# Softmax attention with unnormalised probabilities: the reciprocal row sums travel through DRAM and scale the output as it leaves PSUM

## The reference

```
def attend(qblk):                      # 8 heads, 1024 queries, 1024 keys
    s = jnp.einsum('bhqd,bhkd->bhqk', qblk, k_t).astype(jnp.float32) * scale
    p = jax.nn.softmax(s, axis=-1)
    return jnp.einsum('bhqk,bhkd->bhqd', p.astype(v_t.dtype), v_t)
...
o_b = o_b.transpose(1, 0, 3, 2, 4).reshape(B, S, MLA_HEADS * MLA_V)
```

## Time and profile before

| | before |
|---|---|
| median of 3 runs | 1935.23 us |
| lowest, highest | 1934.19, 1937.03 us |
| the profiled execution's own time | 1936.58 us |
| its span in the trace | 1934.7 us |
| PE busy | 1885.0 us (97%) |
| DVE busy | 1388.8 us (72%) |
| ACT busy | 1066.4 us (55%) |
| chain that ended last | PE 91%, DVE 5%, ACT 2% |

### The profile page before, as it was taken

How to read it: one execution, slowest core, us unless ns; L and a number is a source line. 1 busy time by engine, 2 the same in 40 slices (tenths; PEclk the granted TensorE clock), 3 DMA queues, 4 the chain that set the end, 5 groups by cost and what they waited for, 6 DMA issues and landing times.

```text
span 1934.7 us, 27125 instructions
## 1 busy us (share of the span) xinstructions
PE 1885.0 (97%) x9427; PEld 1598.3 (83%) x9427; DVE 1388.8 (72%) x1941; ACT 1066.4 (55%) x1768; POOL 135.8 (7%) x147
## 2 busy tenths in 40 slices
PE   8999999999999999999999999995999999999998
PEld 8988888888878888888888888884788888888886
DVE  4578777777855656556866348746799898998986
ACT  6576565655552434344534123324677777877775
POOL 1021111011000000000000000000000101001010
PEclk9999999999999999999999999997999999999999
DMA  6110000000321202021353553534999999999993
GB/s 209 44 43 7 23 18 23 23 18 26 121 66 33 64 25 66 22 77 65 120 176 131 178 192 109 175 142 181 359 400 400 391 401 393 396 400 390 399 391 77
DMA packets 147482, 327.58 MB, mean 169 GB/s; under 512 B 18080, under 2 KB 72736, under 8 KB 147232
## 3 DMA queue, kind: packets, MB, share of 16 engines
q1 hardware_dynamic: 141600, 309.59, 43.0%
q0 software_dynamic: 4752, 16.78, 3.4%
q10 hardware_dynamic: 1040, 0.00, 0.0%
HBM read 287.92 MB, written 38.40 MB: 169 GB/s over the span
## 4 chain that ended last, share of the span: by engine, by line
PE 91%; DVE 5%; ACT 2%; issue 1%; DMA 1%; POOL 1%; SPq 0%; DVEq 0%; ACTq 0%; POOLq 0%
PE ps L1108 24%; PE ps L1110 24%; PE ps L1109 24%; PE ps L1097 7%; PE ps L1195 3%; PE ps L1403 1%; PE ps L1234 1%; PE ps L1233 1%; PE ps L1415 1%; PE ps L1387 1%; PE ps L1413 1%; DVE affT L2571 1%; DMA xs<-in_x 1%; DVE top_v L2564 0%; DVE pT_lo L1719 0%
## 5 line engine op out<-in xcount | busy, mean ns | idle before, releaser
L1719 DVE TENSOR_TENSOR w_lo<-w_raw,w_hi 128x1024 fp32r<-128x1024 f32 x384 | 442.7, 1219 | 54.8 <-ACT w_hi L3173 54.6
L3173 ACT ACTIVATE w_hi<-w_raw 128x1024 fp32r<-128x1024 f32 x384 | 371.1, 1053 | 0.4 <-PE ps L1110 0.4
L1108 PE MATMUL ps<-w_hi,xeT_hi 128*128 128x512 f32 x512 | 201.2, 393 | 1.0 <-DVE w_lo L1719 0.9
L1110 PE MATMUL ps<-w_hi,xeT_lo 128*128 128x512 f32 x512 | 199.7, 390 | 0.0
L1109 PE MATMUL ps<-w_lo,xeT_hi 128*128 128x512 f32 x512 | 199.2, 389 | 0.0
L1719 DVE TENSOR_TENSOR d_lo<-d_raw,d_hi 128x1024 fp32r<-128x1024 f32 (+1 forms) x66 | 67.1, 1027 | 124.5 <-ACT d_hi L2814 119.9
L1108 PE MATMUL ps<-hT_parts,d_hi 128*128 128x512 f32 x368 | 145.3, 395 | 0.0
L1110 PE MATMUL ps<-hT_parts,d_lo 128*128 128x512 f32 x368 | 143.9, 391 | 0.0
L1109 PE MATMUL ps<-hT_parts,d_hi 128*128 128x512 f32 x368 | 143.8, 391 | 0.0
L1015 POOL TENSOR_TENSOR stat<-stat,minus_half 128x4 f32<-128x4 f32 (+3 forms) x56 | 54.3, 971 | 1176.5 <-DVE stat L1716 1176.4
L1954 DVE TENSOR_REDUCE row_max<-ps 128x1 f32<-128x1024 f32 x64 | 78.3, 1224 | 79.1 <-PE ps L1234 79.0
(11 more groups left out here) (451 smaller groups left out, 4363.3 us busy)
## 6 DMA issues: line engine op xcount, KB each, us to landing
w_raw<-in_w_gate_e SPq DMA_DIRECT2D x128, 512.0 KB, 7.4
w_raw<-in_w_up_e SPq DMA_DIRECT2D x128, 512.0 KB, 7.1
w_raw<-in_w_down_e SPq DMA_DIRECT2D x128, 512.0 KB, 6.6
d_raw<-in_w_in SPq DMA_DIRECT2D x80, 256.0 KB, 3.3
gates_T<-stage SPq DMA_DIRECT2D x16, 512.0 KB, 2.7
sg<-gates_T SPq DMA_DIRECT2D x16, 512.0 KB, 3.7
stage<-mla_out_T SPq DMA_DIRECT2D x12, 512.0 KB, 5.2
xs<-in_x SPq DMA_DIRECT2D x8, 512.0 KB, 12.8
```

Of the source, the lines that this page charges most:

```text
L1108: pe.matmul(out_ap, a_hi, b_hi, start=start, stop=False)
L1110: return pe.matmul(out_ap, a_lo, b_hi, start=False, stop=stop)
L1719: return dve.tensor_tensor(dst, whole, high.bitcast(F32), ALU.subtract)
L3173: nc.scalar.activation(w_hi[:, n % RING, :], w_raw[:, n % RAW, :], ACT.Copy).then_inc(hi_ok, 1)
```

## The change

The exponentials stay as they are in `probs`. When four tiles of a head are done, DVE takes the reciprocals of their sums in one instruction (`inverse_sums`, 128 x 4). SP writes these 512 numbers to DRAM in query order (`store_inverse`) and reads them back, the same 512 numbers to each of the 128 partitions (`spread_inverse`), into `obS` itself, or for the very last half into a free slot of `probs`. `head_out` then multiplies bank 6 by them instead of copying it. PE's transposes wait for the exponentials instead of the normalised tile. The 64 reciprocals and 64 multiplications of `normalise` are gone, and 16 reciprocals and 32 transfers are added. The one load of `hT_again` (4 MB) becomes eight of 512 KB, each issued when the one before has landed, and the list of SP is written over the same steps.

```diff
+        def inverse_at(h, half):
+            if (h, half) == (MH - 1, 1):
+                return probs[:, (NT * MH - 3) % 3, 0:HALF]
+            return obS[:]
...
-            for i in range(MH):
-                if i + 2 < MH:
-                    load_ukv(i + 2)
...
-                if i:
-                    store_ob(i - 1, 0)
...
-                if i == MH - 1:
-                    sp.wait_ge(h_out, 32)
-                    sp.wait_ge(seam_tr, MH * 8)
-                    sp.dma_start(hT_again, h_dram.rearrange("k p s -> p k s")).then_inc(hT_in, 16)
-                if i:
-                    store_ob(i - 1, 1)
-            load_gla(0, 0)
-            load_gla(0, 1)
-            store_ob(MH - 1, 0)
+            def store_inverse(h, half):
+                m = 2 * h + half
+                sp.wait_ge(inv_ok, m + 1)
+                if m:
+                    sp.wait_ge(inv_in, 16 * m)
+                sp.dma_start(inv_dram[half].rearrange("(t p) -> p t", p=P), row_inv[:, Q4 * half:Q4 * half + Q4],
+                             allow_slow_non_contiguous=True).then_inc(inv_out, 16)
+
+            def spread_inverse(h, half):
+                m = 2 * h + half
+                sp.wait_ge(inv_out, 16 * m + 16)
+                if m and m < 2 * MH - 1:
+                    sp.wait_ge(ob_out, 16 * m)
+                if m == 2 * MH - 1:
+                    sp.wait_ge(p_tr, 2 * (NT * MH - 3) + 2)
+                sp.dma_start(inverse_at(h, half), spread(inv_dram[half], HALF)).then_inc(inv_in, 16)
+
+            def load_rows(k):
+                if k == 0:
+                    sp.wait_ge(h_out, 32)
+                    sp.wait_ge(seam_tr, MH * 8)
+                else:
+                    sp.wait_ge(hT_in, 16 * k)
+                sp.dma_start(hT_again[:, k, :], h_dram[k]).then_inc(hT_in, 16)
...
+                if n == 0 and i:
+                    store_inverse(i - 1, 1)
+                    if i == MH:
+                        spread_inverse(i - 1, 1)
+                if n == 2 and i:
                     store_ob(i - 1, 0)
...
+                    if i < MH:
+                        spread_inverse(i - 1, 1)
+                if n == 4:
...
+                    if i < MH:
+                        store_inverse(i, 0)
+                    if 0 < i < MH:
+                        store_ob(i - 1, 1)
+                if n == 6:
+                    spread_inverse(i, 0)
+                if n == 6 and i == MH - 1:
+                    load_gla(0, 0)
+                    load_gla(0, 1)
+                if n % 2 == 0 and 8 * (MH - 1) + 2 <= 8 * i + n:
+                    for k in range(2):
+                        if 8 * i + n - 8 * (MH - 1) - 2 + k < KD:
+                            load_rows(8 * i + n - 8 * (MH - 1) - 2 + k)
             store_ob(MH - 1, 1)
...
             def probs_T(t):
-                pe.wait_ge(p_ok, t + 1)
+                pe.wait_ge(exp_ok, t + 1)
...
-            def normalise(t):
-                n = t % NT
-                dve.wait_ge(exp_ok, t + 1)
-                s.link(dve.reciprocal(row_inv[:, n:n + 1], row_sum[:, n:n + 1]))
-                dve.tensor_scalar(probs[:, t % 3, :], probs[:, t % 3, :], row_inv[:, n:n + 1], None,
-                                  ALU.mult).then_inc(p_ok, 1)
+            def inverse_sums(h, half):
+                m = 2 * h + half
+                dve.wait_ge(exp_ok, NT * h + Q4 * half + Q4)
+                if m >= 2:
+                    dve.wait_ge(inv_out, 16 * (m - 1))
+                at = slice(Q4 * half, Q4 * half + Q4)
+                dve.reciprocal(row_inv[:, at], row_sum[:, at]).then_inc(inv_ok, 1)
...
             def head_out(h, j):
                 dve.wait_ge(pv_mm, 2 * h + j + 1)
                 if h or j:
                     dve.wait_ge(ob_out, 32 * h + 16 * j)
-                dve.tensor_copy(obS[:], ps[:, 6, :]).then_inc(ob_ev, 1)
+                dve.wait_ge(inv_in, 32 * h + 16 * j + 16)
+                dve.tensor_tensor(obS[:], ps[:, 6, :], inverse_at(h, j), ALU.mult).then_inc(ob_ev, 1)
...
-            END_STEP = (MH - 1, 7)
             for i, n in STEPS:
-                if (i, n) == END_STEP:
-                    probs_low(tile_at(i, n))
+                t = 8 * i + n
                 if i < MH:
                     row_maximum(i, n)
...
+                if 0 <= t - 2 < 8 * MH:
+                    probs_low(t - 2)
+                if n == 0 and i:
+                    inverse_sums(i - 1, 1)
+                if n == 4 and i < MH:
+                    inverse_sums(i, 0)
...
             def rows_high(k):
-                act.wait_ge(hT_in, 16)
+                act.wait_ge(hT_in, 16 * (k + 1))
```

More of the change, by code:

```diff
@@ L518, in hybrid_layer @@
         exp_ok = sem("exp_ok")
-        p_ok = sem("p_ok")
         p_tr = sem("p_tr")
+        inv_ok = sem("inv_ok")
+        inv_out = sem("inv_out")
+        inv_in = sem("inv_in")
         pt_hi = sem("pt_hi")
@@ L618, in hybrid_layer @@
         s_sig = Later(latT_act, 7)
-        g_out = [Later(h_out, 32), Later(hT_in, 16)]
+        g_out = [Later(h_out, 32), Later(hT_in, 16 * KD)]
+        rows_out = Later(inv_out, 32 * MH)
+        ffn_in = Later(inv_in, 32 * MH)
+        f_mm = Later(s_mm, NT * MH)
+        f_ev = Later(exp_ok, NT * MH)
+        x1_sq = Later(max_ok, NT * MH)
         sg_in = [Later(w_uq_in, 16 * MH), Later(w_ukv_in, 16 * MH)]
@@ L1301, in _ @@
                         seam(*seam_at(i, n))
[L1302 to L1303 removed]
+                if 0 <= 8 * i + n - 2 < 8 * MH:
+                    probs_T(8 * i + n - 2)
                 if pv_at(i, n):
@@ L1533, in late_tile @@
                     taken = t - 4 if t < 6 else t - 2
-                    pe.wait_ge(f_ev, 2 * taken + half + 1)
+                    pe.wait_ge(f_ev.sem, f_ev.at(2 * taken + half + 1))
                 for k in rows:
@@ L2018, in _ @@
                         seam_low(*seam_at(i, n))
-                if tile_at(i, n) is not None and (i, n) != END_STEP:
-                    probs_low(tile_at(i, n))
-                if tile_at(i, n + 1) is not None and (i, n) not in (END_STEP, (MH, 0)):
-                    normalise(tile_at(i, n + 1))
-                if (i, n) in ((MH - 1, 6), END_STEP):
-                    normalise(tile_at(i, n + 2))
+                if 0 <= t - 2 < 8 * MH:
[4 more added lines that the diff above has]
+                    inverse_sums(i, 0)
                 if n == 0 and i + 1 < MH:
@@ L2453, in residual @@
             def residual(t, half):
-                dve.wait_ge(f_mm, 2 * t + half + 1)
+                dve.wait_ge(f_mm.sem, f_mm.at(2 * t + half + 1))
                 x = x1[:, t, half * HALF:(half + 1) * HALF]
                 bank = 4 * half + (t if t < 4 else t % 2)
-                dve.tensor_tensor(x, ps[:, bank, :], x, ALU.add).then_inc(f_ev, 1)
+                dve.tensor_tensor(x, ps[:, bank, :], x, ALU.add).then_inc(f_ev.sem, 1)
             def ffn_mean(t):
-                dve.wait_ge(x1_sq, 2 * t + 2)
+                dve.wait_ge(x1_sq.sem, x1_sq.at(2 * t + 2))
                 st.link(dve.tensor_tensor(stat[:, 7, t:t + 1], stat[:, 7, t:t + 1], stat[:, 11, t:t + 1], ALU.add))
@@ L2804, in exponentials @@
                     act.wait_ge(p_tr, 2 * (t - 3) + 2)
+                if i and n % Q4 == 0:
+                    act.wait_ge(inv_ok, 2 * i - 1 + n // Q4)
                 nc.scalar.activation(probs[:, t % 3, :].rearrange("p (a c) -> p a c", a=2),
@@ L2857, in _ @@
                     seam_high(*seam_at(i, n))
-                if tile_at(i, n) is not None:
-                    probs_high(tile_at(i, n))
+                t = 8 * i + n
+                if 0 <= t - 2 < 8 * MH:
+                    probs_high(t - 2)
                 if i < MH:
```

59 lines of the change are left out of this document (29 added, 30 removed).

## The result

| | before | after |
|---|---|---|
| median | 1934.72 us (4 runs) | 1956.72 us (4 runs) |
| lowest, highest | 1934.19, 1937.03 us | 1955.46, 1958.01 us |
| after / before | | 1.0111, 95% interval 1.0094 to 1.0129 |
| profiled execution, own time | 1936.58 us | 1958.01 us |
| its span | 1934.7 us | 1956.1 us |

The change costs about 22 us, 1.1%, outside the range of the prediction. DVE has indeed been relieved of 49.1 us. I went through the trace by the prediction's own list.

What follows compares the result with a forecast made beforehand. The prediction took PE to bound the kernel, DVE having time to spare. The 1.0 us gain is swallowed; 3.7 us of late tile 62 plus 1.7 us of clock give +5.4, 1940.6 us on the median, range 1934.8 to 1942.8.

Steps and rivals of the forecast that it cites:

- What bounds the kernel: Mid-attention PE is busy 48.00 of 48 us and DVE 36, so relieving DVE there shortens nothing.
- what is removed: PE's waits for normalised tiles go (0.7 us), plus 0.3 at the start: PE about 1.0 us earlier at step (7, 7).
- What is added in the middle: In each head, multiplying costs no more than copying; the inverse's round trip, at most 11.6 of 22 us, is hidden: 0.
- The step that failed: Pricing the inverse's store to DRAM by loads of 1024 separate numbers, landing after 3.1 and 4.3 us.
- Row load 2: Near the attention's end, the 512 KB load issued on SP at 509.3 lands at 513.1, delaying the weights.
- SP's queue: Before the first weights, row loads waiting for each other move the first weight load from 510.88 to 514.0: +3.1 us.
- the splits: ACT waits for weights until 520.3; DVE's low part begins at 521.35, and the two splits take 2.3 us, to 523.7.
- DVE's order: Near the end DVE takes tile 63's row maximum before tile 61's low parts, delaying tile 62's transposes: +1.2 us.
- my sum: Whole kernel: 3.7 us later at tile 62's transposes plus 1.7 us of slower clock, +5.4 us.
- The clock: After PE idles 5.1 us before tile 62's transposes, the granted clock falls to 0.66 for a while, costing 1.7 us.
- The last round trip: Rival, chance 0.10: four queued transfers make head 7's first-half store land 2 us late for the last head_out; 1942 to 1945.
- The fixed cost: By the skill page's about 2.0 us per transfer, the inverse's store and spread would take 4 us, hidden mid-attention.

Runs made afterwards that it cites:

- e5: The kernel before with normalise removed and nothing in its place, transposes waiting for the exponentials; 1934.31 us, ratio 0.9992.
- e2: The changed kernel with the inverse stored as 128 runs of four numbers instead of 512 single ones, so outputs get wrong inverses; 1941.34 us, ratio 1.0027.
- e3: The changed kernel with the inverse's stores issued from ACT's queue instead of SP's; 1958.98 us, ratio 1.0122.
- e1: The changed kernel with the first weights' four loads issued ahead of the inverse's store and the row loads; 1947.01 us, ratio 1.006.
- e4: The changed kernel without any inverse: no reciprocals, stores or spreads of them, head_out copies; 1938.51 us, ratio 1.0018.
- e7: The changed kernel with e2's 16-byte store plus a second store of 512 single numbers 64 bytes apart, the spread awaiting both; 1941.76 us, ratio 1.0036.
- e8: e6 with the 16-byte store of e2, so each inverse goes to another query; 1934.11 us, ratio 0.999.
- e9: e8 with inverses in their right places: DVE picks every fourth number, multiplying bank 6 in place and copying, except the last half; 1934.23 us, ratio 0.9991.
- e6: The changed kernel, slow store kept: one 4 MB row load, weights and last stores issued earlier, tile 61's low parts first on DVE; 1942.71 us, ratio 1.004.

## Why the prediction was wrong, point by point

- **What bounds the kernel, what is removed**: right. e5 puts the worth of the removed work at 0.8 us by the medians, 2.7 by the spans; I had taken 1.0.
- **What is added in the middle**: right in its answer, wrong in its price. With 8.0 us for the store and the 5.0 of a held store of `obS` the sum that I bounded by 11.6 us is 8.0 + 5.0 + 5.1 = 18.1, and the 22 us of cover still hide it.
- **The step that failed** is "A store of 512 separate numbers is bounded by the loads of 1024 separate numbers, which land after 3.1 and 4.3 us". It measured 8.0. A load writes to SBUF and reads DRAM; the row said nothing on writing neighbouring words of DRAM, and I gave the term an upper end from it all the same. From this came the second error: I priced the store only in the places where someone waits for its own numbers. In "Row load 2 follows at 509.3 ... 513.1" I added 0.5 us for the 256 KB store ahead and nothing for the inverse's store, which is issued at 508.62, before both. It made row load 2 land at 521.9 instead (e2, with the store made cheap: at about 513.4; e3: late again from another queue). That alone is 8.8 of the 12.9 us at tile 62.
- **SP's queue, the splits, DVE's order**: right, as e2 shows, where only the store was made cheap: weights issued at 514.28 (forecast 514.0), ACT's split at 520.90 (520.3), PE at 526.28 (525.6). DVE's order is 1.17 us in e1 (1.2). e2's ratio of 1.0027 is +5.2 us; my sum was +5.4, and some luck is in that. In e2's profiled execution tile 62 is 4.4 us late (I had 3.7) and the slower clock costs 2.0 (I had 1.7), so that the gate products are 6.5 us late; some 1.6 of that come back because the clock then stayed up (next point), which I had not counted on.
- **The clock**: right in kind. Behind the 14.26 us wait PE ran at 0.50 from 535 to 540 us and lost 2.5 us by the end of the attention, where I had 1.7. The Trainium skill ("TensorE: Matmul & The Clock Gate", "What's actually happening") has the reduced rate as the default that activity releases, and the fall agrees. But I took the fall behind the 1.93 us wait of the earlier trace rows for what such a wait does, and it isn't: behind waits of 1.93 to 2.00 us before the same gate products the clock fell to 0.50 in the kernel before, e4, e5 and e7 and stayed at 1.00 in e2, e8 and e9. From the first pair of gate products to the second it is 4.9 us in the kernel before and 3.3 in e2, e8 and e9.
- **The last round trip**, a rival with a chance of 0.10 and 2 us, came true with all its four transfers: the inverse's store took 8.0 us and of the 20.3 us by which the last `head_out` is late, 12.9 came from tile 62, 2.5 from the clock and the remaining 4.9 from here. The inverse's store took 8.0 us where the rival had 4.3, row load 6 took 6.8 where it had 5.1, and the store of half 0 took 4.2 where 2.2 are usual. The slack of "3 us or so" would not have covered it: in e1 the last inverse's store is issued at 528.71, as early as I had forecast, and tile 62 is only 0.3 us late, and still the last multiplication starts at 548.44, 10.7 us after the copy of before.
- **The fixed cost** of about 2.0 us in the Trainium skill ("DMA: Bandwidth & Descriptors", "Anatomy of one DMA"), which that section gives for the path of transfers that GpSimd issues, while SP and ACT issue these: the 16-byte runs (1.4 us median) and the single numbers 64 bytes apart (2.8) are near it, the neighbouring single numbers (8.0) are not. The measurement decides.

What stays open: why single writes to neighbouring words finish so late with the transfer engines idle, and what exactly they hold. e3 shows that it isn't the queue; whether transfers of every kind are held was not tried. The stores of `obS` (11.4 us in the changed kernel, 5.4 in e6) are stores that were, the row loads are loads that were, and e6's second weight load may be one that was issued first and held all the same.

## What to carry to other kernels

A few bytes written in the wrong pattern can be the dearest transfer of a kernel: before a tiny scattered store enters a chain, look for a row of a scattered *store*, not of a load, or measure one, and count what is issued behind it as waiting too, also on another queue. Give each partition a run of its own, even of 16 bytes, and let the reader undo the order. Work taken off an engine that has 12 of 48 us to spare was worth 0.8 us here, no more than could be told from nothing, so the new transfers and the new order of the queues are the whole effect of such a change: read those first.

## What the runs showed of the hardware

- The landing time of a 2 KB store to DRAM from 128 partitions: 8.0 us as 512 neighbouring single numbers (its packets moved within some 0.5 us; 8.2 to 10.3 in e3, e1 and e6, with other transfers beside it in the last two), 2.8 us as 512 single numbers 64 bytes apart, 1.4 us as 128 runs of 16 bytes.
- While such a store was unfinished the transfer engines moved 8 GB/s for 6 us (the stretch 512 to 518) though a 512 KB load had been issued 1 us after it; the load landed after 12.3 us, 4.7 in e2. The same happened with the store on another engine's queue (11.4 us). A 256 KB store issued 0.6 us after it landed after 11.4 us, 3.7 in e2.
- DVE multiplied a 128 x 512 PSUM bank by an SBUF operand in 0.68 us when that was read in order, and in 1.07 us when it took every fourth number of it.
- Behind a wait of 1.9 to 2.0 us of PE the granted clock fell to 0.50 in four profiled executions and stayed at 1.00 in three.
